# First projection section of a two-layer encoder on the input before its norm, its rows scaled on the copy out, the input turned tile by tile

## What is computed

```python
def rmsnorm(x, g, eps=1e-6):
    return x * rsqrt(mean(x * x, axis=-1) + eps) * g

xn = rmsnorm(x, norm_mix[0])
h = xn @ ab_w_in[0]
a_q, a_f, a_i, a_g, b_q, b_k, b_v, b_g, b_lr = split_cols(h, AB_SIZES)
```

## Time and profile before

| | us |
|---|---|
| median of 3 runs | 1491.38 (1487.81 to 1494.68) |
| the profiled execution, its own time | 1490.56 |
| its span in the profile | 1488.8 |
| PE busy, share of the span | 1421.9, 96% |
| DVE, ACT, POOL busy | 545.7, 549.2, 590.2 |

### The profile page before, as it was taken

One profiled execution on the slowest core, in us unless ns is written; L12 is line 12 of the kernel. 1 busy time (PEld: TensorE's weight loads), 2 busy tenths in 40 slices (PEclk: granted clock), 3 DMA queues, 4 the chain that ended last, 5 costly groups with the idle time before them and its releaser, 6 DMA issues.

```text
span 1488.8 us, 27322 instructions
## 1 busy us (share of the span) xinstructions
PE 1421.9 (96%) x11099; PEld 1330.1 (89%) x11103; DVE 545.7 (37%) x1039; ACT 549.2 (37%) x887; POOL 590.2 (40%) x303
## 2 busy tenths in 40 slices
PE   4999999899999999999999988989999999999998
PEld 3788899799999999999988765947999999999997
DVE  5124655534331223122417975152342213311324
ACT  4325565434432233122454244153343223421232
POOL 1332223133545244434435255373344534453442
PEclk9999999999999999999999999999999999999999
DMA  4221122142333223322332320201222322232221
GB/s 144 73 84 47 54 63 67 51 117 79 90 93 100 71 85 88 110 71 67 85 84 83 71 89 1 79 1 29 86 85 85 103 81 80 84 104 71 81 74 60
DMA packets 208774, 114.34 MB, mean 77 GB/s; under 512 B 16692, under 2 KB 202936, under 8 KB 208696
## 3 DMA queue, kind: packets, MB, share of 16 engines
q1 hardware_dynamic: 203448, 109.50, 25.5%
q10 hardware_dynamic: 5248, 3.73, 0.8%
HBM read 107.26 MB, written 5.96 MB: 76 GB/s over the span
## 4 chain that ended last, share of the span: by engine, by line
PE 61%; issue 23%; POOL 9%; DVE 6%; ACT 1%; POOLq 0%; DVEq 0%; ACTq 0%
PE ps L984 55%; POOL w_lo L535 6%; POOL arena L519 2%; DVE arena L1814 2%; PE ps L1079 2%; DVE m_only L1809 2%; PE ps L1310 1%; PE ps L1350 1%; PE ps L1322 1%; POOL m_only L519 1%; DVE arena L1797 1%; DVE small L1829 1%; DVE arena L1778 0%; ACT arena L848 0%; PE ps L1453 0%
## 5 line engine op out<-in xcount | busy, mean ns | idle before, releaser
L535 POOL TENSOR_TENSOR w_lo<-w_raw,w_hi 128x1024 fp32r<-128x1024 f32 x202 | 498.5, 2471 | 815.5 <-ACT w_hi L598 815.5
L984 PE MATMUL ps<-x_hi,w_hi 128*128 128x272 f32 (+1 forms) x1952 | 408.1, 290 | 6.2 <-POOL w_lo L535 3.2
L984 PE MATMUL ps<-x_hi,w_lo 128*128 128x272 f32 (+1 forms) x1952 | 405.2, 289 | 0.0
L984 PE MATMUL ps<-x_lo,w_hi 128*128 128x272 f32 (+1 forms) x1952 | 403.8, 288 | 0.0
L984 PEld LDWEIGHTS ps<-x_hi,w_hi 128*128 128x128 f32 (+1 forms) x1952 | 307.0, 188 | 12.7 <-issue 7.3
L984 PEld LDWEIGHTS ps<-x_lo,w_hi 128*128 128x128 f32 (+1 forms) x1952 | 307.0, 188 | 0.5
L984 PEld LDWEIGHTS ps<-x_hi,w_lo 128*128 128x128 f32 (+1 forms) x1952 | 305.2, 189 | 0.5
L598 ACT ACTIVATE w_hi<-w_raw 128x1024 fp32r<-128x1024 f32 x202 | 211.1, 1050 | 193.3 <-PE ps L984 144.4
L984 PE MATMUL ps<-o_hi,w_hi 128*128 128x272 f32 x960 | 200.5, 290 | 2.0 <-DVE arena L1693 1.1
L984 PE MATMUL ps<-o_hi,w_lo 128*128 128x272 f32 x960 | 199.9, 290 | 0.0
L984 PE MATMUL ps<-o_lo,w_hi 128*128 128x272 f32 x960 | 199.1, 289 | 0.0
(11 more groups left out here) (242 smaller groups left out, 1398.1 us busy)
## 6 DMA issues: line engine op xcount, KB each, us to landing
w_raw<-in_ffn_w_in SPq DMA_DIRECT2D x88, 512.0 KB, 3.7
w_raw<-in_ffn_w_out SPq DMA_DIRECT2D x32, 512.0 KB, 3.7
w_raw<-in_ab_w_in SPq DMA_DIRECT2D x28, 512.0 KB, 3.8
w_raw<-in_cd_w_in SPq DMA_DIRECT2D x13, 512.0 KB, 3.7
w_raw<-in_ffn_w_out SPq DMA_DIRECT2D x16, 384.0 KB, 3.4
w_raw<-in_ab_w_out SPq DMA_DIRECT2D x8, 512.0 KB, 4.1
arena<-in_x_prompt SPq DMA_DIRECT2D x4, 512.0 KB, 5.2
w_raw<-in_cd_w_in SPq DMA_DIRECT2D x8, 256.0 KB, 3.4
```

The lines of the kernel that those rows point to most:

```text
L535: pool.tensor_tensor(wl[:, s, :], raw[:, s, :], wh[:, s, :].bitcast(F32), ALU.subtract).then_inc(lo_done, 1)
L984: mm = pe.matmul(ps[0:M, b + h, 0:HALF], w[:, s, k * M:(k + 1) * M], xs[x][:, k, h * HALF:(h + 1) * HALF], start=(begin and k == ks[0] and ...
```

## The change

The first section no longer waits for the norm. Since the norm's factor is one number for each token, and the section's output has tokens on the partitions, the section can multiply x times g, split in high and low parts in the buffers `oh` and `ol`, and each row of the output is multiplied by its token's factor `rcol` as ACT copies it out. In the diff:

1. PE first makes 36 matmuls of the identity with itself. It then transposes each prompt tile as it lands (7 of the 8 k; the eighth has no bank yet), then the parameters, then the sample tile. The eighth k is turned within the section, behind its first k.
2. The parameters are 7 transfers in place of 10, issued by ACT.
3. ACT (`first_x`) copies two of the turned tiles, and makes the high parts of x times g, with the high parts of chunks 0 to 3 between them; DVE copies the others and makes the low parts (`first_lo`).
4. PE's `first_section` is the old section with its loops changed (pass outside token tile). Behind k = 4 it makes the norm's products, now with five small ones more that give the sum as a column for each token tile. ACT's `rms(0, 0)` makes `rstd` as before, and `rcol` from the five columns with two more Ln and two more Exp.
5. ACT's and DVE's `first_norm()`, which fill `xh` and `xl`, stand behind that, and now `C_LR` is the first job to wait for `xh` and `xl`.

```diff
-    order = [("x", k) for k in range(KT)] + [0, C_LR]
+    order = ["norm0", 0, C_LR]
...
+            def first_x():
+
+                off = 0
+                for src, n in rows:
+                    act.dma_start(par_in[off:off + n, :], src).then_inc(s_par, 16)
+                    off += n
+                for k in (0, 2):
+                    act.wait_ge(x_turned, k + 1)
+                    act.activation(xT[:, k, 0:TP], ps[:, 4 + k, :], ACT.Copy).then_inc(xc_act, 1)
+                act.wait_ge(s_part, 2)
+                for k in range(KT):
+                    if k in (0, 2):
+                        act.wait_ge(xc_act, k // 2 + 1)
+                    act.wait_ge(xc_dve, X_COPIED[k])
+                    act.activation(oh[:, k, :], xT[:, k, :], ACT.Copy, scale=pc("mix0", k)).then_inc(raw_hi, 1)
+                    if k % 2 == 0:
+                        hi(k // 2)
...
-                rms(0)
+                rms(0, 0)
...
-                if n in (2, 4):
+                if n in (0, 2, 4):
+                    key = "norm" if n else "norm0"
                     for m, i0, i1 in token_tiles:
...
-            for c in range(LEAD):
-                hi(c)
+            first_x()
             first_norm()
-            hp = [LEAD]
+            hp = [SLOTS]
...
-            take_values(0, 0)
+            take_values(0, 0, rcol)
...
+            for _ in range(36):
+                pe.matmul(ps[:, 3, 0:P], ident[:, :], ident[:, :], start=True, stop=True)
+            for i in range(NT):
+                pe.wait_ge(x_landed[i], 16)
+                for k in range(KT - 1):
+                    mm = pe.transpose(ps[:, X_BANK[k], i * P:(i + 1) * P], x_in[:, i, k * P:(k + 1) * P], ident[:, :])
+                    if i == NT - 1:
+                        mm.then_inc(x_turned, 1)
+            pe.wait_ge(s_par, 16 * len(rows))
+            pe.transpose(ps[:, 3, 2 * P:2 * P + NPR], par_in[0:NPR, :], ident[0:NPR, 0:NPR]).then_inc(s_part, 1)
+            pe.wait_ge(x_landed[NT], 16)
+            pe.wait_ge(s_part, 2)
             for k in range(KT):
...
+            def first_section():
+
+                bank_free = [(xc_act, 1), (xc_dve, 1), (xc_act, 2), (xc_dve, 2), (xc_dve, 4)]
+                for q in range(KT // 2):
+                    pe.wait_ge(hi_done, q + 1)
+                    for kk in range(2):
+                        k = 2 * q + kk
+                        pe.wait_ge(raw_lo, k + 1)
+                        for a, (w, x) in enumerate(PASSES):
+                            if a == 2 and kk == 0:
+                                pe.wait_ge(lo_done, q + 1)
...
+                        if k == 0:
+                            turn_last_x()
+                        if k == 4:
+                            pe.wait_ge(xc_dve, 7)
+                            norm(0, 0)
+                    mm.then_inc(chunk_done, 1)
...
-            tm_section(0, AH * ADV, ready=xready(0))
-            job(C_LR, X0, M=RANK)
+            first_section()
+            job(C_LR, X0, M=RANK, ready=xready(0))
...
+            first_copy(1)
+            first_copy(3)
+            dve.wait_ge(s_part, 1)
+            dve.tensor_copy(par[:, 0:NPR], ps[:, 3, 2 * P:2 * P + NPR]).then_inc(s_part, 1)
+            dve.wait_ge(x_turned, KT)
+            dve.tensor_copy(xT[:, :, TP:T], ps[:, 3, 0:KT * TS].rearrange("p (k t) -> p k t", k=KT)).then_inc(xc_dve, 1)
+            dve.wait_ge(s_part, 2)
+            first_copy(4)
+            first_lo(0)
```

More of the change, by code:

```diff
@@ L269, in build @@
         rows, prow = [], {}
[L270 to L275, removed]
+        for names, src, n in [(("mix0", "mix1"), I["norm_mix"], 8), (("ffn0", "ffn1"), I["norm_ffn"], 8), (("final",), I["norm_final"], 8),
+                              (("lb0", "lb1"), I["hgrn_lb_logits"], 4), (("ga",), I["hgrn_gnorm"], 1), (("gb",), I["gla_gnorm"], 1),
+                              (("bgk",), I["gla_b_gk"], 2)]:
+            at = sum(r[1] for r in rows)
+            for j, name in enumerate(names):
+                prow[name] = at + j * n
+            src = src.rearrange("l (k p) -> (l k) p", p=P) if len(src.shape) == 2 else src.rearrange("(k p) -> k p", p=P)
+            rows.append((src, n * len(names)))
         NPR = sum(r[1] for r in rows)
@@ L469, in _ @@
             for i in range(NT):
-                sp.dma_start(x_in[:, i, :], I["x_prompt"][0, i * P:(i + 1) * P, :]).then_inc(s_in, 16)
-            sp.dma_start(xs_in, I["x_sample"][0]).then_inc(s_in, 16)
-            for c in range(LEAD):
[L473 to L478, removed]
+                sp.dma_start(x_in[:, i, :], I["x_prompt"][0, i * P:(i + 1) * P, :]).then_inc(x_landed[i], 16)
+            sp.dma_start(xs_in, I["x_sample"][0]).then_inc(x_landed[NT], 16)
+            for c in range(SLOTS):
                 load(c)
@@ L761, in head_hi, with take_values @@
                 act.activation(oh[:, unit(u)[2][e][3], :], osb, ACT.Copy).then_inc(o_hi, 1)
-            def take_values(c0, v0):
+            def take_values(c0, v0, rows=None):
                 for c in range(c0, c0 + 4):
@@ L768, in take_values @@
                 for i in range(NT):
-                    act.activation(val[:, i, v0:v0 + 512], ps[:, 4 + i, :], ACT.Copy).then_inc(s_val, 1)
-                act.activation(val[0:TS, NT, v0:v0 + 512], ps[0:TS, 2 * (jof[c0] % 2), :], ACT.Copy).then_inc(frees(c0), 1)
+                    act.activation(val[:, i, v0:v0 + 512], ps[:, 4 + i, :], ACT.Copy, scale=rows[:, i:i + 1] if rows is not None else 1.0)\
+                       .then_inc(s_val, 1)
+                act.activation(val[0:TS, NT, v0:v0 + 512], ps[0:TS, 2 * (jof[c0] % 2), :], ACT.Copy,
+                               scale=rows[0:TS, NT:NT + 1] if rows is not None else 1.0).then_inc(frees(c0), 1)
             act.wait_ge(s_lb, 2)
             act.activation(cm[:, 4:12], cm[:, 4:12], ACT.Exp).then_inc(s_lb, 1)
-            take_values(0, 0)
+            take_values(0, 0, rcol)
             ahead(C_LR)
@@ L996, in _ @@
                 for i in range(NT):
[L997 to L1004, removed]
+                    mm = pe.transpose(ps[:, 3, i * P:(i + 1) * P], x_in[:, i, (KT - 1) * P:KT * P], ident[:, :])
@@ new lines, in turn_last_x @@
+                mm.then_inc(x_turned, 1)
+            def first_section():
[8 more added lines that the diff above has]
+                                pe.wait_ge(lo_done, q + 1)
+                            for i in range(NT + 1):
+                                if k == 0 and a == 0:
+                                    pe.wait_ge(*bank_free[i])
+                                out = ps[:, 4 + i, :] if i < NT else ps[0:TS, 2 * (jof[0] % 2), :]
+                                mm = pe.matmul(out, (oh, ol)[x][:, k, i * P:min(T, (i + 1) * P)], w[:, q, kk * 512:(kk + 1) * 512],
+                                               start=(k == 0 and a == 0), stop=(k == KT - 1 and a == 2))
+                        if k == 0:
[4 more added lines that the diff above has]
+                    mm.then_inc(chunk_done, 1)
```

56 lines of the change are left out of this document (31 added, 25 removed).

## The result

Over 20 executions of each kernel on one chip the median went from 1493.87 us (1487.81 to 1498.80) to 1496.54 us (1493.85 to 1499.67). The ratio is 1.0021, with a 95% interval of 1.0012 to 1.0031: the changed kernel is slower by about 3 us, less than the 0.5% that was called no change ahead of the run. The forecast was 2.5 us more. The sum comes out; its parts, as the rows show, only in part.

The account below looks back on a forecast made before the run. PE bounds the kernel, full from 32.66 to C_LR's end at 68.8. C_LR starting 0.3 us late plus 2.2 for its low clock make 2.5 us more: 1493.1 profiled, 1493.9 median, verdict same; 8-in-10 range 1487 to 1501.

Parts of the forecast that it names:

- The step that decides: Before C_LR: chunk 4's high part waits behind ACT's norm work, so PE waits from 53.0 to 63.1, 10.1 us.
- N: Within the first section: the time at which the norm's sum is ready behind k = 4, forecast at 42.8 us.
- The start: Kernel start: identity matmuls end at 12.8, transposes, copies and first high parts take 7.85, section starts at 20.7, not 32.66.
- C_LR's clock: C_LR behind PE's pause: about 4.9 us at the low clock, so C_LR ends 2.2 us later; bounds nothing to 5.9.
- The rival by which C_LR runs low to its end: C_LR: its 16 columns don't raise the clock, 6.2 us later in all, 1497.6 us; chance 0.15.
- The rival by which it never falls: Clock stays high before the section and before C_LR, 2.3 and 2.2 us go, 1489.4 us; chance 0.13.
- the same in both kernels and hangs on C_LR's end: Everything behind C_LR: claimed alike in both kernels, following C_LR's end through PE and ACT, so no cost of its own.
- The squares: Within the section: copies of k = 1 to 7 and squares over by about 35, before they are asked for at 39.
- second rival: Kernel start: identity matmuls don't raise the clock and end at 17.9; 8.4 us more, 1502.3 us; chance 0.12.
- turning tiles as they land gives nothing by itself: Kernel start: identity matmuls end at 12.8, later than x's landing at 10.2, so only the high clock for transposes is won.
- The faster case: Before C_LR: chunk 4's weights are not late, C_LR ends at 59.9 instead of 68.8, about 1483 us; chance 0.09.
- The weighing of a page: ACT's table switches behind the norm: trace gives 1.3 us each, page 2.66; page's rule means 1498.0 us, chance 1 in 100.

Follow-up runs that it names:

- e1: Changed kernel with the high parts of chunks 4 and 5 made by ACT ahead of the norm's rstd; ratio to the kernel before 0.9985, 5.4 us less than the changed kernel.
- e10: Changed kernel again, unchanged, for a second profile; C_LR starts at 61.86 us and the key job at 71.42.
- second pair: Second profiles of the kernel before and the changed kernel, both unchanged; key job starts at 70.60 us in the former, 71.42 in the latter.
- e2: Changed kernel without the 36 identity matmuls; ratio to the kernel before 1.0006, 2.2 us less than the changed kernel, uncertain by 2.7.
- e11: Changed kernel with POOL's low parts of chunks 1 to 3 held until DVE's low parts of x are made; ratio to the kernel before 1.0020.
- e12: Changed kernel with six unused identity products behind the second section, ahead of the first key transposes; ratio to the kernel before 0.9997, 3.6 us less than the changed kernel.
- e3: Changed kernel with 42 unused identity products filling PE's pause between the section and C_LR; ratio to the kernel before 0.9998, 3.4 us less than the changed kernel.
- e4: Kernel before with only the 36 identity matmuls added ahead of its wait for x, results unused; ratio to the kernel before 1.0003.
- e6: Changed kernel with chunks 4 and 5 prepared ahead of the norm and its Ln and Exp grouped, saving two table loads; ratio to the kernel before 0.9949.

## Why the prediction was right

**The step that decides.** The prediction said that ACT reaches chunk 4 only behind the norm, that the last low part of x ends at N + 16.3, that the low part of chunk 4 begins 1.6 us behind it and takes 2.4, and that PE waits 10.1 us with POOL's w_lo as releaser. Measured: 40.8 + 16.3 = 57.1, then 1.62, then 2.40, and 9.71 us of waiting. e1 removes exactly this wait by moving two high parts ahead of the norm. So the mechanism is shown. Of the section's head start of 13.4 us, 9.7 go into this wait, 2.0 into the transposes and norm's products that now stand in the section, and 1.7 are left at C_LR's start.

**The start was 1.4 us better than forecast** (19.29 for 20.7). PE was through with the identity matmuls at 12.04, not 12.8, and the eight transposes of the sample tile took 0.65 us where 0.9 and their signal were charged. The first is partly luck of this execution: in e10 they ended at 12.81, and the section started at 20.05. Up to the norm's products at 38.72 the section took 19.4 us, of which 75 matmuls at 0.2275 and 0.5 for the transposes are 17.6; so the low clock at its start cost 1.9 us at most, where 2.3 were charged. The norm's products took 2.0, not 2.2. Together N was 2.0 us earlier, and C_LR began at 61.10, not 63.1: **1.7 us ahead of before, not 0.3 behind**; in the second pair 0.7 ahead (61.86 for 62.60).

**C_LR's clock.** Charged were 2.2 us, measured 2.72, in the second pair of profiles 1.56 (9.56 against 8.00), and 1.2 to 1.8 in e2, e11 and e12, which have the same pause (9.50, 9.78 and 9.23). e3 shows that it is the pause. The rival by which C_LR runs low to its end is refused: the clock rose within it, at 67.12. The rival by which it never falls is refused too.

**The term that was missing.** At the key job the changed kernel is 1.0 us behind, in the second pair 0.8, and in e12 it is 0.4 ahead of the first profile of before; the forecast had 2.5. So most of the 2.7 between the medians lies behind the key job, where the prediction said "the same in both kernels and hangs on C_LR's end". The instructions are the same, but not their clock: 10.2 us at the lower level in both profiles of the changed kernel, 3.4 in both of before. So the total was right by luck, by two errors that cancel: about 1.5 us too much at C_LR and as much too little behind it. How much of the difference of the medians the low stretches make is not shown, as e4 has 10.2 us of them with a ratio of 1.0003. e12 speaks for a part, since a few products at the later pause brought the ratio down by 3.6 us, half of it seen behind the key job. The price of a low stretch is in the table above; what sets its place and length is open: with the same program before the key job they still fell at other times.

**The squares** were said to be done by about 35. They ended at 38.55 (32.86 + 5.69), just before the products at 38.72 that need them, because DVE's low parts of x were held up by POOL. It cost nothing here, by 0.2 us; in e11 it did.

**The identity matmuls** raised the clock, as forecast and against the second rival; but e2 shows them to be no help: 9.9 us of PE's time buy 28 transposes in 3.22 us instead of 5.55, when the tiles are there from 4.6 us on. In e2 the clock rose at 8.60 under the transposes alone, which the second rival doubted (its 3.3 us are 30 transposes at 0.11, not the 36 that it names). That "turning tiles as they land gives nothing by itself" is true only behind them.

**The faster case** had 0.09. It did not happen, but its mechanism is e1's: with the weights ready C_LR started at 51.66 and ended at 58.5, behind the last low part of x, and not at the 59.9 forecast there. What that rival missed was the next wait, 4.07 us for ACT's copy of C_LR's result; it was called "below 1".

**Copies with a scale** were said to cost what those without do. L786 took 0.68 us each with a scale (59.5 to 61.2) and 0.60 without (112.0 to 113.4), so val's four cost 0.3 us more. C_LR hid that here.

**The weighing of a page.** The Trainium skill (ScalarE: Activation LUTs, What ACT_TABLE_LOAD costs) has 2.66 us for each switch. The changed kernel's load begins at 41.56, as Ln ends, and the next one at 43.53 with an Exp of 0.66 between: 1.31 us for the switch. The trace doesn't agree with the page, and e6, which saved two loads, gained 2.47 us at the first low part of x. Two switches at the page's figure would be 5.3, an estimate that this does not bear out.

## What to carry to other kernels

When a section is moved ahead of the work that it used to wait for, list what each engine's program order still holds behind that work: here one weight chunk, behind ACT's norm, took back 9.7 us, and two lines that moved it won 5.4 us (uncertain by 2.5). Bring the consumer's inputs forward in the same edit, then look for the next copy in line (e1's 4.07 us). And where PE stands for some microseconds, charge the clock behind it: look up the time at the lower level in each stretch, 0.4 us lost for each microsecond here. Don't expect the total of one profile to tell effects of 2 or 3 us, since low stretches elsewhere move by as much.

## What the runs showed that was not expected

**DVE and POOL hold each other up.** DVE's low part of x takes 0.79 us alone and 2.3 to 2.9 beside POOL; POOL's low part of a chunk takes 2.40 us alone and 2.89 beside DVE, while DVE's copies out of PSUM kept their 0.68. DVE's timeline, and POOL's group of the same stretch (shortest, median and longest in ns):

```profile
18.32 0.79 DVE L1526 SCALAR_TENSOR_TENSOR o_lo<-xT,par,o_hi 128x544 fp32r<-128x544 f32 x1 [0.30 <-ACT o_hi L614]
...
19.91 2.38 DVE L1526 SCALAR_TENSOR_TENSOR o_lo<-xT,par,o_hi 128x544 fp32r<-128x544 f32 x1 [0.20 <-ACT o_hi L614]
22.21 0.68 DVE L1521 COPY xT<-ps 128x512 f32<-128x512 f32 x1
22.81 2.33 DVE L1526 SCALAR_TENSOR_TENSOR o_lo<-xT,par,o_hi 128x544 fp32r<-128x544 f32 x1
```

```profile
L535 POOL TENSOR_TENSOR w_lo<-w_raw,w_hi x4: 2387/2891/2897, 19.3 to 27.4; 128x1024 fp32r<-128x1024 f32 x4
```

e11 shows the cause by parting them: the median of the low parts falls from 1556 to 780 ns. The Trainium skill (SBUF — State Buffer, Who interferes with whom) says that an operation of VectorE with two inputs in SBUF contends with one of GpSimd that reads SBUF, and calls the contention an exclusive lock. The trace agrees: POOL's first ends at 19.3 + 2.39 = 21.7, and the DVE operation that started during it, at 19.91, ends at 22.29, 0.6 us behind it.

**The moment at which the clock rises moves.** The identity matmuls began at 2.30. The windows of the changed kernel:

```profile
0.00:5.68 5.68, 3.38 (x16) 3.38 (x17) 0.00 (x0) 1.28 (x1) 2.71 (x16) 1.00 0.67 231
5.68:12.00 6.32, 6.32 (x58) 6.32 (x58) 0.00 (x0) 0.00 (x0) 0.00 (x0) 1.00 1.03 358
```

Up to 5.68 a pass took 3.38/16 = 0.21 us, behind it 6.32/58 = 0.11, the two levels; the clock column says 1.00 for both, as it did in the earlier trace rows at 32.60. So the clock rose 3.4 us after the work began, not 5.3, and eight products were slow instead of twelve. In the other seven profiles with these products at the start it rose 3.6 to 5.6 us after it, at 5.88 (e12) to 7.91 (e3), so the forecast's 5.3 was not off: this profile is the earliest of eight.
